# First modulation in column halves, a new order of two blocks, and two edits in the first attention

## The reference

```
mod = silu(c) @ w_ada + b_ada
sh1, sc1, g1, sh2, sc2, g2 = split(mod, 6)
h = rms_norm(x, norm1_g) * (1 + sc1) + sh1
proj = h @ w_in
...
o, l = dilated_window_attention(qa, ka, va, win, dil)   # 12 heads in 3 groups
...
x = x + g1 * (mixed @ w_out)
```

## Time and profile before

| | |
|---|---|
| median of three runs | 1816.92 us |
| the profiled execution | 1816.28 us |
| its span | 1814.2 us |
| TensorE busy | 1778.0 us (98%) |
| VectorE busy | 1349.9 us (74%) |
| ScalarE busy | 949.5 us (52%) |
| mean granted TensorE clock | 0.999 |

### The profile page before, as it was taken

One profiled execution on the slowest core, in us unless ns is written; L12 is line 12 of the kernel. 1 busy time (PEld: TensorE's weight loads), 2 busy tenths in 40 slices (PEclk: granted clock), 3 DMA queues, 4 the chain that ended last, 5 costly groups with the idle time before them and its releaser, 6 DMA issues.

```text
span 1814.2 us, 25435 instructions
## 1 busy us (share of the span) xinstructions
PE 1778.0 (98%) x9988; PEld 1519.4 (84%) x9988; DVE 1349.9 (74%) x1881; ACT 949.5 (52%) x1035; POOL 201.8 (11%) x173
## 2 busy tenths in 40 slices
PE   8999999999999999999999999999999999999998
PEld 3787757899999988888888888798979888888886
DVE  5679688589499966665666666758974779898897
ACT  2543574544454444444444444457644667667665
POOL 0000000388500024440000000000000000000000
PEclk9999999999999999999999999999999999999999
DMA  8655654555355568885555555554344688898894
GB/s 319 251 189 185 227 217 182 215 187 204 140 203 182 214 223 291 294 287 206 194 196 185 185 186 191 183 209 169 134 153 164 237 327 336 332 354 336 319 352 175
DMA packets 65552, 414.34 MB, mean 228 GB/s; under 512 B 8769, under 2 KB 9057, under 8 KB 19121
## 3 DMA queue, kind: packets, MB, share of 16 engines
q1 hardware_dynamic: 51904, 371.22, 55.6%
q0 software_dynamic: 7504, 25.80, 4.2%
q10 hardware_dynamic: 6050, 16.02, 2.2%
HBM read 395.45 MB, written 16.78 MB: 227 GB/s over the span
## 4 chain that ended last, share of the span: by engine, by line
PE 86%; DVE 7%; DMA 3%; ACT 2%; issue 1%; SPq 0%; DVEq 0%; ACTq 0%
PE ps L2442 23%; PE ps L2444 22%; PE ps L2443 22%; PE ps L2828 6%; PE ps L2857 3%; PE ps L2830 3%; DVE wlo L1320 2%; DMA BIG<-in_stream_dram 1%; ACT whi L758 1%; PE ps L3040 1%; DMA raw<-in_stream_dram 1%; DVE BIG L1405 1%; PE ps L2918 1%; DVE H L1359 1%; PE ps L2549 0%
## 5 line engine op out<-in xcount | busy, mean ns | idle before, releaser
L1320 DVE TENSOR_TENSOR wlo<-raw,whi 128x2048 fp32r<-128x2048 f32 x181 | 414.6, 2291 | 207.3 <-ACT whi L758 207.2
L758 ACT ACTIVATE whi<-raw 128x2048 fp32r<-128x2048 f32 x181 | 346.8, 1916 | 367.7 <-PE ps L2444 241.9
L2442 PE MATMUL ps<-whi,phi 128*128 128x512 f32 x608 | 237.7, 391 | 2.3 <-DVE plo L1927 2.3
L2443 PE MATMUL ps<-wlo,phi 128*128 128x512 f32 x608 | 236.6, 389 | 0.0
L2444 PE MATMUL ps<-whi,plo 128*128 128x512 f32 x608 | 236.6, 389 | 0.0
L2442 PE MATMUL ps<-whi,tboth 128*128 128x512 f32 (+1 forms) x576 | 226.5, 393 | 7.1 <-DVE wlo L1320 3.9
L2442 PE MATMUL ps<-tboth,whi 128*128 128x256 f32 x768 | 221.0, 288 | 2.9 <-DVE tboth L1342 2.8
L2444 PE MATMUL ps<-whi,tboth 128*128 128x512 f32 (+1 forms) x576 | 222.9, 387 | 0.0
L2443 PE MATMUL ps<-wlo,tboth 128*128 128x512 f32 (+1 forms) x576 | 222.6, 386 | 0.0
L2444 PE MATMUL ps<-tboth,wlo 128*128 128x256 f32 x768 | 217.2, 283 | 0.0
L2443 PE MATMUL ps<-tboth,whi 128*128 128x256 f32 x768 | 217.2, 283 | 0.0
(11 more groups left out here) (442 smaller groups left out, 3287.2 us busy)
## 6 DMA issues: line engine op xcount, KB each, us to landing
raw<-in_stream_dram SPq DMA_DIRECT2D x243, 1024.0 KB, 4.8
BIG<-in_stream_dram SPq DMA_DIRECT2D x90, 1024.0 KB, 6.6
BIG<-g_spill POOLq DMA_DIRECT2D x64, 128.0 KB, 4.7
s_spill<-MOD ACTq DMA_DIRECT2D x28, 256.0 KB, 2.0
late_units<-in_stream_dram SPq DMA_DIRECT2D x6, 1024.0 KB, 5.7
H<-in_stream_dram SPq DMA_DIRECT2D x6, 1024.0 KB, 4.8
BIG<-in_stream_dram SPq DMA_DIRECT2D x2, 2048.0 KB, 16.3
g_spill<-H ACTq DMA_DIRECT2D x4, 1024.0 KB, 5.4
```

Of the source, the lines that this page charges most:

```text
L758: nc.scalar.activation(hi_of(u), raw_of(u), ACT.Copy).then_inc(unit_hi, 1)
L1320: nc.vector.tensor_tensor(wlo[:, u % 2, :], raw_of(u), whi[:, u % 2, :].bitcast(f32), ALU.subtract).then_inc(unit_split, 1)
L2442: nc.tensor.matmul(out, ahi, bhi, start=start, stop=False)
L2443: nc.tensor.matmul(out, ahi, blo, start=False, stop=False)
```

## The change

The eight `w_ada` chunks are loaded in column halves, all lower halves first, then `first_w` (now to `MOD`, where it overwrites nothing), then the upper halves, with block 1's lower unit between chunks 3 and 4 and block 0's upper unit behind them. The two units change places: `DC+2` is now the one with number `U_IN + 1`. TensorE takes chunks 1, 3, 4, 6 for the lower half and 1, 3 for the upper, VectorE the others. Upper rows of the modulation go to banks 6 and 7. TensorE multiplies block 0 lower (both tiles) and block 1 lower before it transposes the upper half of `h`. The transposes use two banks in place of four and so wait for low parts. GpSimd's broadcast waits for three units. In the first attention the exp table is loaded by a small activation ahead of copy `QKT_FIRST`, and the values go to banks 6 and 3 in turn (5 for the last), so `a_values(i)` waits for i - 1 outputs and no longer for i; `b_scores(0)` and `b_scores(1)` wait for five and six outputs. The diff, cut to what the text speaks of:

```diff
-        ADA_LOADS = ((0, 1), (1, 2), (2, 4), (4, 6), (6, 7))
-        ADA_BY_DVE, ADA_BY_PE = (0, 2, 5, 6), (1, 3, 4)
+        ADA_LOADS = ((0, 1), (1, 2), (2, 4), (4, 6), (6, 7), (7, 8))
+        ADA_BY_PE = (1, 3, 4, 6), (1, 3)
...
+        def ada_landed(c, h):
+
+            first, last = ADA_LOADS[ada_in[c]]
+            return ada_loaded[ada_in[c]], 16 * (last - first) * (h + 1)
...
-        first_shift, first_scale = ([ps[:, 2 * h + k, :] for h in range(2)] for k in range(2))
+        first_shift, first_scale = ([ps[:, 6 * h + k, :] for h in range(2)] for k in range(2))
...
-        first_w = ada_raw[0]
+        first_w = MOD[:, UW:2 * UW]
...
+        def a_bank(i):
+
+            return 6 if i % 2 == 0 else 5 if i == A_SLOTS * TT - 1 else 3
...
+            if t == T_H1:
+                return 4 + k % 2
...
-            for k, (first, last) in enumerate(ADA_LOADS):
-                if last - first == 1:
-                    sp.dma_start(ada_raw[first], stream[first, :, :]).then_inc(ada_loaded[k], 16)
-                else:
-                    sp.dma_start(big[:, first * UW:last * UW].rearrange("p (a n) -> p a n", n=UW),
-                                 stream[first:last, :, :].rearrange("a p n -> p a n")).then_inc(ada_loaded[k], 16)
-                if last == 4:
-                    sp.dma_start(X[:, :, :], io["x"].rearrange("(t p) d -> p t d", p=P)).then_inc(x_loaded, 16)
             for h in range(2):
-                sp.dma_start(both_halves(ada_raw[7], h), both_halves(stream[7:8, :, :].rearrange("a p n -> (a p) n"), h)
-                             ).then_inc(ada_loaded[ada_in_7 + h], 16)
-            sp.wait_ge(ada_summed, 1)
-            sp.dma_start(first_w, stream[DC, :, :]).then_inc(raw_loaded[0], 16)
-            sp.dma_start(raw[:, 1, :], stream[DC + 1, :, :]).then_inc(raw_loaded[1], 16)
+                for k, (first, last) in enumerate(ADA_LOADS):
+                    if h:
+                        sp.wait_ge(ada_loaded[k], 16 * (last - first))
+                    for c in range(first, last):
+                        sp.dma_start(both_halves(ada_raw[c], h),
+                                     both_halves(stream[c:c + 1, :, :].rearrange("a p n -> (a p) n"), h)
+                                     ).then_inc(ada_loaded[k], 16)
+                    if last == 4 and h == 0:
+                        sp.dma_start(X[:, :, :], io["x"].rearrange("(t p) d -> p t d", p=P)).then_inc(x_loaded, 16)
+                    if last == 4 and h == 1:
+                        sp.dma_start(raw[:, 1, :], stream[DC + 2, :, :]).then_inc(raw_loaded[1], 16)
+                if h == 0:
+                    sp.dma_start(first_w, stream[DC, :, :]).then_inc(raw_loaded[0], 16)
             sp.wait_ge(raw_loaded[0], 16)
-            sp.dma_start(raw[:, 0, :], stream[DC + 2, :, :]).then_inc(raw_loaded[0], 16)
+            sp.dma_start(raw[:, 0, :], stream[DC + 1, :, :]).then_inc(raw_loaded[0], 16)
             sp.wait_ge(unit_split, 1)
             sp.dma_start(raw[:, 1, :], stream[DC + 3, :, :]).then_inc(raw_loaded[1], 16)
...
-            pool.wait_ge(unit_used, 2)
+            pool.wait_ge(unit_used, 3)
...
                     "p (c t) -> p c t", c=4), ACT.Copy).then_inc(h1_copied, 1)
+            tr_high(T_H1, 0, (0, 1))
             hi(U_IN + 1, 0, in_at(1), 0)
-            for k in H1_ORDER:
-                chunks, tokens = tr_place(T_H1, k)
-                act.wait_ge(tr_done, k + 1)
-                nc.scalar.activation(thi[:, chunks, tokens], ps[:, tr_bank(T_H1, k), :].rearrange(
-                    "p (c t) -> p c t", c=4), ACT.Copy).then_inc(tr_hi, 1)
+            tr_high(T_H1, 0, (2, 3))
             hi(U_IN + 2, 0, in_at(2), 0)
...
-                    evac(2 * b + t, min(U_IN + 2 * b + 1, U_PA - 1), proj[:, t, 512 * b:512 * b + w], width=w)
...
+                    evac(2 * b + t, min(U_IN + max(2 * b + 1, 2), U_PA - 1), proj[:, t, 512 * b:512 * b + w], width=w)
...
-                if b:
+                if b > 1:
                     in_high(2 * b + 2)
                 in_high(2 * b + 3)
+                if b == 0:
+                    in_high(4)
                 in_out(b)
...
-            for g in range(0, QKT_FIRST + 2, 2):
+            for g in range(0, QKT_FIRST, 2):
                 qkT_copy(g)
+            nc.scalar.activation(warm, pidx, ACT.Exp, scale=0.0)
+            qkT_copy(QKT_FIRST)
             a_exp(0)
             for g in range(QKT_FIRST + 2, QKT_ALL, 2):
                 qkT_copy(g)
...
+            def first_sum(h, c, ends=False):
+
+                dve.wait_ge(*ada_landed(c, h))
+                total, part = both_halves(ada_acc[0], h), both_halves(ada_raw[c], h)
+                if c == 0:
+                    last = nc.vector.tensor_scalar(total, part, siluc[:, c:c + 1], None, ALU.mult)
+                else:
+                    settle()
+                    last = nc.vector.scalar_tensor_tensor(total, part, siluc[:, c:c + 1], total, ALU.mult, ALU.add)
+                if ends:
+                    last.then_inc(ada_summed, 1)
+                else:
+                    mark(last)
...
+            def first_modulated(h):
+
                 dve.wait_ge(ada_full, h + 1)
...
+            first_sum(0, 0)
+            first_sum(0, 2)
+            norm(0, X, None)
+            first_sum(0, 5)
+            first_sum(0, 7, True)
+            first_modulated(0)
+            first_sum(1, 0)
+            first_sum(1, 2)
+            tr_low(T_H1, 0, (0, 1))
+            first_sum(1, 4)
+            first_sum(1, 5)
             lo(U_IN + 1)
-            for n, k in enumerate(H1_ORDER):
-                chunks, tokens = tr_place(T_H1, k)
-                dve.wait_ge(tr_hi, n + 1)
-                nc.vector.tensor_tensor(tlo[:, chunks, tokens], ps[:, tr_bank(T_H1, k), :].rearrange(
-                    "p (c t) -> p c t", c=4), thi[:, chunks, tokens].bitcast(f32), ALU.subtract).then_inc(tr_lo, 1)
+            first_sum(1, 6)
+            first_sum(1, 7, True)
+            first_modulated(1)
+            tr_low(T_H1, 0, (2, 3))
...
-                nc.vector.tensor_scalar(oa[:, t, h * HD:(h + 1) * HD], ps[:, 6, 0:HD], a_rec[:, b:b + 1], None,
+                nc.vector.tensor_scalar(oa[:, t, h * HD:(h + 1) * HD], ps[:, a_bank(i), 0:HD], a_rec[:, b:b + 1], None,
...
+                        if t == T_H1 and k >= 2:
+                            pe.wait_ge(tr_lo, k - 1)
...
+            def first_ada(h, c):
+
+                pe.wait_ge(*ada_landed(c, h))
+                for m in (h, 2 + h):
                     nc.tensor.matmul(first_rows[m], silu_cols[:, c, :], ada_raw[c][:, m * 512:(m + 1) * 512],
...
+            def first_spread(h):
+
+                pe.wait_ge(ada_summed, h + 1)
                 for m in (h, 2 + h):
                     last = nc.tensor.matmul(first_rows[m], ones, ada_acc[0][:, m * 512:(m + 1) * 512],
                                             start=False, stop=True)
                 last.then_inc(ada_full, 1)
+
+            for c in ADA_BY_PE[0]:
+                first_ada(0, c)
+            first_spread(0)
+            first_ada(1, ADA_BY_PE[1][0])
...
             first_rows_part(0)
+            first_rows_part(1)
+            first_ada(1, ADA_BY_PE[1][1])
+            first_spread(1)
+            for t in range(TT):
+                pe.wait_ge(tr_lo, t + 1)
+                rows_part(2, U_IN + 1, 0, t, at=in_at(1))
             transposes(T_H1, H, (2, 3))
-            first_rows_part(1)
-            for t in range(TT):
-                pe.wait_ge(tr_lo, t + 1)
-                rows_part(0, U_IN, 1, t, at=in_at(0))
-            pe.wait_ge(tr_lo, 4)
-            block_rows(2, U_IN + 2, at=in_at(2))
+            for t in range(TT):
+                pe.wait_ge(tr_lo, 3 + t)
+                rows_part(0, U_IN + 1, 1, t, at=in_at(1))
+            for t in range(TT):
+                rows_part(2, U_IN + 2, 1, t, at=in_at(2))
...
             def a_values(i):
                 t, h, b = i // A_SLOTS, i % A_SLOTS, i % 2
-                if i:
-                    pe.wait_ge(a_out, i)
-                else:
+                if i >= 2:
+                    pe.wait_ge(a_out, i - 1)
+                elif i == 0:
                     pe.wait_ge(v_moved, 16 * CLASSES * TT)
                 pe.wait_ge(a_trT, i + 1)
...
                     pe.wait_ge(a_masked, n_a - 1 + h)
+                    pe.wait_ge(a_out, n_a - 3 + h)
```

More of the change, by code:

```diff
@@ L155 @@
 ROWS = {t: sum(2 * TT if k in HALVED else TT for k in range(t + 1) if k != T_OA) for t in range(10)}
-H1_ORDER = (2, 3, 0, 1)
 T_GROUPS = [4, 1, 4, 4, 4, 4, 4, 2, 4, 4]
@@ L419, in hybrid_block_then_mixer_memory_moe_kernel @@
         siluc_ready, ones_ready = sem("siluc_ready"), sem("ones_ready")
-        ada_loaded, ada_summed = [sem(f"ada_loaded{k}") for k in range(len(ADA_LOADS) + 2)], sem("ada_summed")
+        ada_loaded, ada_summed = [sem(f"ada_loaded{k}") for k in range(len(ADA_LOADS))], sem("ada_summed")
```

(26 more changed lines are left out.)

22 lines of the change are left out of this document (removed).

## The result

| | before | changed |
|---|---|---|
| median of seven runs each | 1817.19 us | 1822.85 us (1821.21 to 1823.78) |
| the profiled execution | 1816.28 us | 1823.44 us |
| its span | 1814.2 us | 1821.3 us |
| mean granted TensorE clock | 0.999 | 0.996 |

The ratio is 1.0028 [1.0018, 1.0037]: the changed kernel is 5.7 us slower. The forecast was +1.5 us, 1818.4, with a range up to 1821.8; the result lies outside it. Runs were taken in batches, and the kernel before ran in each: its medians were 1817.19 us (beside the changed kernel), 1816.95 (attention alone, modulation alone, early split, long filling), 1816.67 (shorter filling, small loads first, both with all orders mended) and 1817.41 (the other four). A ratio compares within a batch; medians of two batches can differ by some 0.7 us for this reason alone.

What follows compares the result with a forecast made beforehand. TensorE, busy 98% of the span, was taken as the bound. Terms +2.9 - 0.7 - 0.7 = +1.5 us on the profiled 1816.28, with the median 0.64 higher: 1818.4 us; 8-in-10 range 1815.4 to 1821.8.

Steps and rivals of the forecast that it cites:

- the clock: TensorE's clock through the first modulation: main forecast took it as steady, with no time lost to a fall.
- the milestone: TensorE finishing first modulation, block 0 and block 1 lower: 53.46 us before, forecast 56.35, 2.9 us later.
- the landings: Weight halves arriving at the start: 0.42 to 0.43 MB per us, x at 12.5 us, c5 upper at 29.8.
- The stall: TensorE before block 0 upper, near 46 us: stands 5.0 us until VectorE's low part ends at 50.6.
- the attention: First attention: table load moved, start 0.83 us sooner, new wait costs 1.0; net -0.7 us (bounds -1.3 and +0.2).
- Rival 2: Upper halves land late, at 300 GB/s after first_w: c5 upper at 33.9 us, +3.9, total 1822.3; chance 0.08.
- The lower half's modulation: VectorE's first modulation starts at 24.1 us, TensorE setting the pace; 5.8 us sooner than before.
- The middle: Between the lower half's modulation and the spread: TensorE waits 1.4 us for VectorE's sums, done at 37.3.
- Rival 1: Clock falls in the new stall: 2.05 us, at most 5.4; total 1820.5, up to 1823.8; chance 0.22.
- the new wait: Attention, b_scores(0) waits for VectorE's fifth output: TensorE 1.0 us later.
- What follows: Three units behind block 0 upper, a load beside the broadcast: wait 1.1 us against 1.8 lost before, 0.7 given back.

Runs made afterwards that it cites:

- attention alone: Kernel before with the two attention edits only (table load moved, values in two banks); 1815.85 us, ratio 0.9994.
- modulation alone: Changed kernel with the attention as it was before, so only the modulation part of the change; 1823.27 us, ratio 1.0037.
- early split: Changed kernel with block 0 upper's split ahead of the upper transposes' copies, and its low part ahead of theirs; 1822.72 us, ratio 1.0032.
- long filling: Changed kernel with 20 dummy float32 products on TensorE behind the upper transposes, in the wait of 5.0 us; 1827.24 us, ratio 1.0054.
- shorter filling: Changed kernel with ten dummy float32 products on TensorE behind the upper transposes, in the wait of 5.0 us; 1824.53 us, ratio 1.0039.
- small loads first: The early split, with ScalarE also issuing its five small loads ahead of that split; 1818.40 us, ratio 1.0009.
- all orders mended: Changed kernel with sums, block 0 upper's split and small loads earlier, block 1 lower's load later, upper transposes between its two tiles; 1815.23 us, ratio 0.9991.
- the other four: Sums first; table load alone; changed kernel with later broadcasts, 1822.55 us; kernel before with both attention edits and later broadcasts, 1814.74 us.
- sums first: Changed kernel with block 1 lower loaded behind all upper halves, and VectorE's last upper sums before that unit's low part; 1819.10 us, ratio 1.0010.
- table load alone: Kernel before with only the exp table load moved, attention values still in one bank; 1816.33 us, ratio 0.9997.
- the orders mended and the broadcasts later: Kernel with all orders mended, GpSimd's two broadcast loads starting after seven and ten used units; 1810.97 us, ratio 0.9966.

## Why the prediction was wrong, point by point

Two steps failed: the clock, taken as steady where it fell twice (4.4 us of the milestone), and the landings, taken too early (2.25 us). The stall itself and the attention came as forecast.

**Landings: the rate was too high at the start.** I carried 0.42 to 0.43 MB per us over to loads in halves. Stretches, before and then changed:

```profile
2.50:5.00 2.50, 0.00 (x0) 0.00 (x0) 0.00 (x0) 0.56 (x1) 0.29 (x1) 1.00 0.96 391
```

```profile
2.50:5.00 2.50, 0.61 (x1) 0.49 (x2) 0.69 (x1) 2.45 (x4) 0.29 (x1) 1.00 0.90 196
5.00:7.50 2.50, 2.50 (x4) 1.00 (x3) 0.75 (x1) 0.00 (x0) 0.00 (x0) 1.00 1.01 372
```

The DMA engines are nearly as busy, yet bring half in the first stretch. The queue of the weights from 2.5 to 5 us (packets, MB, share of 16 engines), before and then changed:

```profile
q1 hardware_dynamic: 121, 0.97, 93.2%
```

```profile
q1 hardware_dynamic: 241, 0.48, 88.4%
```

Its packets are 2 KB instead of 8 KB. Share times 16 engines times 2.5 us over the packets gives 147 ns for one here, and in the same way 84 ns from 5 to 7.5 us, against 308 ns for 8 KB (four times 84 is 336, 9% more for each byte). The Trainium skill ("DMA: Bandwidth & Descriptors", Why small descriptors are slow) gives each packet a fixed cost of some three cycles. By that I estimate 2 KB to be 3.5% slower for each byte than 8 KB; this trace shows more. So x landed at 14.38 (forecast 12.5), 1.9 us late, and c5 upper at 32.09 (29.8), 2.3 late. The one stretch I took the rate from was the last chunk of the kernel before, late in the stream. Rival 2, which I held at 0.08, had the consequence right (late upper halves delay all behind them, 2.25 us instead of 3.9) but not the place: it put the slow rate behind first_w, where 402 to 423 GB/s were moved from 15 to 35 us; most of the lateness arose before x. Why 2 KB packets are slow only at the start is open, and no run tested the size of the packets by itself.

The lower half's modulation at 24.27 hit the forecast (24.1) by luck. The late x made VectorE's sum end at 22.19 instead of 20.0; TensorE, which was to set the pace until 22.2, was done at 20.8, as its first product came at 4.4 us instead of 6.2, and waited for the sum:

```profile
22.25 1.98 PE L2599 MATMUL ps<-MID,BIG 128*128 128x512 f32 x4 [1.47 <-DVE MID L1436]
```

**The middle: the wait was 3.1 us, not 1.4**, and ends with the sums at 39.55 instead of 37.3: the same 2.3 us. The mended order shows that it needed no faster load: 0.7 us in "sums first", 1.6 and 0.5 in the two kernels with all orders mended.

**The clock: twice, where I had it steady.** From the end of the sums to VectorE's modulation I allowed 2.2 us (37.3 to 39.5), and 3.75 passed: +1.55. From the end of the low part (54.43) to the milestone block 0 upper took 8.6 us instead of 5.75: +2.85. Rival 1 priced one fall at 2.05 and gave it 0.22; two happened. This is the step that failed with the most weight. In the profiles of this study the clock fell behind the wait of 3.0 to 3.1 us in six kernels of seven, and behind that of 5 us in all four that left it empty. Of three other waits this long it fell behind two (3.9 us in the early split, 3.0 in the shorter filling) and not behind the 3.51 us of the orders mended. The argument against ("products just before are dense, the clock stayed at 1.00") came from a trace whose longest wait was 1.6 us, and such a trace has nothing to say on longer ones. The Trainium skill's page ("TensorE: Matmul & The Clock Gate", HAM oscillation) did say that idle gaps bring the clock down. The odds were mine: even in the text, less in the chances. The page was the better guide; the traces agree with it in 12 of the 14 waits of 3 us or more that stand behind the kernels' start.

**The stall: right.** 4.95 us, released by the low part, against 5.0.

The milestone by these terms: 56.35 + 2.25 + 1.55 + 2.85, and 0.04 in the steps between, is 63.04.

**What follows: right, for a part.** The lag shrank by 0.87 (0.7 forecast), but the rows have it in two moves, -2.0 and +1.1, and the second is the broadcast's: it is absent where only the broadcasts start later.

**The attention: right.** VectorE's loop starts 0.79 us sooner against the lag (0.83 forecast); the table load stands ahead of its copy; the new wait is 1.10 us (1.0 forecast):

```profile
211.29 1.28 ACT L929 ACT_TABLE_LOAD   x1
212.58 0.20 ACT L929 ACTIVATE SM<-SM 128x1 f32<-128x1 f32 x1
213.36 0.60 ACT L920 ACTIVATE MID<-ps 128x512 f32<-128x512 f32 x1 [0.57 <-PE ps L2658]
```

```profile
238.82 1.13 PE L2711 MATMUL ps<-MID 64*128 64x256 f32 x8 [1.10 <-DVE BIG L1676]
```

The lag goes from 8.72 to 8.23 there, -0.5 for -0.7. Behind it a chain of two loads was 1 us shorter than in the profile of before; the kernel with the modulation alone has some of this too, so at least a part of it does not come from the attention's edits; the rest is not explained.

**The range** was short at the top because I let rivals 1 and 2 exclude each other. They share a cause: a late sum makes the wait long, and the clock fell behind long waits. Their prices add: 1818.4 + 2.05 + 2.05 + 2.25 is 1824.8, and the changed kernel stands at 1822.85.

What stays open: why the clock stayed up behind two waits of fourteen (3.1 us in the shorter filling, 3.51 in the orders mended), why it fell behind some waits of only 1.2 to 1.3 us, and why it fell for 3.4 us in some executions and 6.8 in others.

## What to carry to other kernels

When an order is changed at the start of a kernel that TensorE bounds, a new wait of 3 us or more costs its length and, in 12 cases of the 14 here, 1.6 to 2.9 us of lower clock behind it: price the two as one event. An engine's list has to be read for everything queued behind the step that moves, small loads and casts included; here the early split gained nothing until the small loads were moved too, and the broadcasts took about 3 us of what the mended orders had gained. And a large transfer that nobody needs soon should be released by a later event than the one it happens to follow: the earlier the kernel gets there, the more such a transfer takes back.

## What the runs showed of the hardware

- Loads in 2 KB pieces: 84 ns a piece against 308 ns for 8 KB; from 2.5 to 5 us 147 ns, and 196 GB/s where 8 KB pieces brought 391.
- The granted clock can fall behind a wait of 1.2 to 1.3 us as well, among small products (table load alone, 238.40 to 240.00: 0.50; modulation alone from 245 us; shorter filling near 1188 us), and can stay up behind one of 3.51 us (orders mended, 60 to 75 us: 1.00); behind the wait of 0.7 us in the mended middle it did not fall.
- Runs of one kernel spread by different amounts: 0.6 us over five runs with the orders mended and the broadcasts later, 5.0 over eleven runs of the kernel that kept one wait of 3 us. But the kernel before, whose longest wait behind its start is 1.6 us, spreads over 4.8 in sixteen runs, so the long waits are not all of it.
- In the first 17 us float32 passes stand 0.86 us apart, as they do at a granted clock of 0.52 later (39.60 to 43.10 in the changed kernel), while the clock's column reads 1.00 there: at the start the distances tell more than that column.
